# First block of a two-block transformer kernel: memory projections placed first, mixed heads in pairs, last modulation chunks in the feed-forward

## The reference

```python
mod = silu(c) @ w_ada + b_ada                      # 6 x 1024: shift1, scale1, gate1, shift2, scale2, gate2
h = rms_norm(x, g_norm1) * (1 + scale1) + shift1
sb_q, sb_k, sb_v, gq, gk, gv, gg, gf = split(h @ w_in)         # 3 x 512, 2 x 256, 2 x 512, 16
# stick-breaking, for each of 8 heads of 64, s < t:
z = q k^T / 8
weights = exp(log_sigmoid(z) + reverse exclusive cumsum over s of log_sigmoid(-z))
o_sb = weights @ v
# gated linear attention, chunks of 64, 4 heads: state = decay * state + k_dec^T v;  o = q state
o_gla = rms_norm(o_gla) * g_gla_out * silu(gg)
x = x + (1 + gate1) * (concat(o_sb, o_gla) @ w_out)
h2 = rms_norm(x, g_norm2) * (1 + scale2) + shift2
u = causal_depthwise_conv(h2 @ w_up); val, gte = split(u)
x = x + (1 + gate2) * ((val * silu(gte)) @ w_down)
# second block, used later:  mkv = rms_norm_2(mem, mem_norm_g) @ mem_kv   for layers a and b
```

## Time and profile before

| | us |
|---|---|
| median of 3 runs | 1300.62 (1298.9 to 1304.4) |
| profiled execution | 1301.19 |
| its span | 1299.4 |
| PE busy | 1150.4 (89%) |
| DVE busy | 803.2 (62%) |
| ACT busy | 547.0 (42%) |
| mean granted clock of PE | 0.944 of full speed |
| chain that ended last: PE, DVE, ACT | 74%, 14%, 7% |

### The profile page before, as it was taken

One profiled execution on the slowest core, in us unless ns is written; L12 is line 12 of the kernel. 1 busy time (PEld: TensorE's weight loads), 2 busy tenths in 40 slices (PEclk: granted clock), 3 DMA queues, 4 the chain that ended last, 5 costly groups with the idle time before them and its releaser, 6 DMA issues.

```text
span 1299.4 us, 24238 instructions
## 1 busy us (share of the span) xinstructions
PE 1150.4 (89%) x10670; PEld 1073.2 (83%) x10670; DVE 803.2 (62%) x1268; ACT 547.0 (42%) x768; POOL 28.4 (2%) x28
## 2 busy tenths in 40 slices
PE   3789998899999977778768999999899779999997
PEld 3789887899999976566657899999788558999997
DVE  6787665678875555655553456655666875455554
ACT  1443441456554445433332444444535224444432
POOL 0000000000000000223000000000000000000000
PEclk9988997889999988888998899999899898999999
DMA  9655553635544442110002355446315203355451
GB/s 358 231 193 195 195 194 132 238 117 194 178 139 169 165 187 100 70 60 2 36 28 73 118 196 181 159 157 205 109 41 196 98 1 130 132 192 185 134 181 54
DMA packets 30233, 185.88 MB, mean 143 GB/s; under 512 B 3360, under 2 KB 4528, under 8 KB 12720
## 3 DMA queue, kind: packets, MB, share of 16 engines
q1 hardware_dynamic: 30128, 184.34, 39.9%
HBM read 183.27 MB, written 1.05 MB: 142 GB/s over the span
## 4 chain that ended last, share of the span: by engine, by line
PE 74%; DVE 14%; ACT 7%; issue 4%; DMA 1%; SPq 0%; DVEq 0%; ACTq 0%
PE banks L308 45%; PE banks L1056 13%; ACT whi L276 3%; DVE wlo L285 3%; PE banks L305 2%; PE banks L460 1%; DMA X<-in_xT 1%; DVE ub L447 1%; DVE adac L1244 1%; PE banks L1575 1%; PE banks L1558 1%; PE banks L1234 1%; DVE ub L367 1%; PE banks L1543 1%; ACT ssb L329 0%
## 5 line engine op out<-in xcount | busy, mean ns | idle before, releaser
L285 DVE TENSOR_TENSOR wlo<-raw,whi 128x2048 fp32r<-128x2048 f32 (+4 forms) x174 | 340.5, 1958 | 215.2 <-ACT whi L276 213.6
L276 ACT ACTIVATE whi<-raw 128x2048 fp32r<-128x2048 f32 (+4 forms) x174 | 285.2, 1640 | 162.7 <-PE banks L1056 97.1
L308 PE MATMUL banks<-h_hi,whi 128*128 128x256 f32 x1632 | 237.3, 299 | 27.8 <-ACT h_hi L356 16.9
L308 PEld LDWEIGHTS banks<-h_hi,whi 128*128 128x128 f32 x1632 | 216.9, 199 | 39.0 <-issue 22.6
L308 PE MATMUL banks<-h_hi,wlo 128*128 128x256 f32 x1632 | 221.5, 290 | 2.5 <-DVE wlo L285 2.5
L308 PE MATMUL banks<-h_lo,whi 128*128 128x256 f32 x1632 | 214.6, 284 | 0.0
L308 PEld LDWEIGHTS banks<-h_hi,wlo 128*128 128x128 f32 x1632 | 210.1, 197 | 4.9 <-DVE wlo L285 2.8
L308 PEld LDWEIGHTS banks<-h_lo,whi 128*128 128x128 f32 x1632 | 202.4, 190 | 3.1 <-issue 2.1
L1056 PE MATMUL banks<-m_hi,whi 128*128 128x256 f32 x528 | 71.3, 281 | 4.9 <-ACT m_hi L1096 4.9
L1086 ACT ACTIVATE u<-u 128x256 f32<-128x256 f32 x44 | 18.4, 418 | 130.2 <-DVE u L1133 130.2
L1056 PE MATMUL banks<-m_hi,wlo 128*128 128x256 f32 x528 | 71.1, 283 | 0.0
(11 more groups left out here) (454 smaller groups left out, 1387.6 us busy)
## 6 DMA issues: line engine op xcount, KB each, us to landing
raw<-in_ada SPq DMA_DIRECT2D x24, 1024.0 KB, 4.9
raw<-in_w_up SPq DMA_DIRECT2D x22, 1024.0 KB, 4.8
raw<-in_a_gu SPq DMA_DIRECT2D x22, 1024.0 KB, 4.8
raw<-in_b_gu SPq DMA_DIRECT2D x22, 1024.0 KB, 4.8
raw<-in_w_in SPq DMA_DIRECT2D x12, 1024.0 KB, 5.9
raw<-in_w_down SPq DMA_DIRECT2D x16, 704.0 KB, 4.1
raw<-in_a_in SPq DMA_DIRECT2D x11, 1024.0 KB, 4.8
raw<-in_a_down SPq DMA_DIRECT2D x16, 704.0 KB, 4.1
```

What stands on the lines that cost most here:

```text
L276: act.activation(hi_s[k % NSPLIT][:, 0:w], raw[n % NRAW][:, 0:w], ACT.Copy).then_inc(*hi_made.tick(k))
L285: dve.tensor_tensor(lo_s[s][:, 0:w], raw[n % NRAW][:, 0:w], hi_s[s][:, 0:w].bitcast(F), SUB).then_inc(*lo_made.tick(k))
L308: i_ = pe.matmul(b[0:m, j * T:(j + 1) * T], a[:, kt * step + j * m:kt * step + j * m + m], x[:, kt, :], start=st, stop=sp)
```

## The change

- **Order of the stream and the projections.** The memory, its gain and the constants `ones` and `eps` are issued first; the four memory chunks head `ONE` (c = 0 to 3), mixed with ada 0 to 7. Then come w_in chunks 0, 2, 4, 7, w_gf, 8, 9, 6, 1, 3, 5, 10, 11 (c = 4 to 16). The first eight scaled chunks use the buffer of the gated state S1 in place of `ub`.
- **Loops.** DVE now splits chunk c+2 first and then scales ada c+3, in loops 5 to 16. `ONE_EXTRA` tells behind which piece the small matmuls stand.
- **Heads in pairs.** z, c and o handle two heads (384 columns each, 768 in all); one double bank holds scores and running sums of a pair, and a matmul with the mask replaces the multiply by `strict`. c waits for DVE's step of the same pair (`("max", p)`). Outputs go from the banks straight to `mm_hi` and `mm_lo`.
- **Gated attention.** It uses two banks only (4 and 5), go alternates between the halves, the gain is folded into the norm.
- **Evacuations.** ACT takes all banks but those of w_gf and w_in 7, 10, 11.
- **Last modulation chunks.** ada 19 is in loop 16, ada 20 to 23 (gate2) stand in the stream behind w_up 2, 6, 10, 14 and are scaled by DVE in those steps of the feed-forward; gate2 is added up at w_up 18.

The diff, cut to its core:

```diff
-WIN = [7, 12, 8, 9, 6, 0, 2, 4, 1, 3, 5, 10, 11]
+WIN = [0, 2, 4, 7, 12, 8, 9, 6, 1, 3, 5, 10, 11]
...
 def stream_order():
-    o = [("ada", i) for i in range(8)]
-    one = [("w_gf", 0) if i == 12 else ("w_in", i) for i in WIN]
-    one += [("mkv_a", 0), ("mkv_a", 1), ("mkv_b", 0), ("mkv_b", 1)]
-    o += one[:6]
-    for j in range(11):
-        o += [("ada", 8 + j), one[6 + j]]
-    o += [("ada", j) for j in range(19, 24)]
-    for name in ("w_out", "w_up", "w_down", "a_in", "a_out", "a_gu", "a_down", "kv_down", "b_in",
+    o = [("mkv_a", 0), ("mkv_a", 1), ("ada", 0), ("ada", 1), ("mkv_b", 0), ("ada", 2), ("ada", 3), ("mkv_b", 1)]
+    o += [("ada", j) for j in range(4, 8)]
+    one = [("w_gf", 0) if i == 12 else ("w_in", i) for i in WIN] + [("w_out", 0)]
+    o += one[:2]
+    for j in range(12):
+        o += [("ada", 8 + j), one[2 + j]]
+    o += [("w_out", i) for i in range(1, 4)]
+    for i in range(22):
+        o.append(("w_up", i))
+        if i % 4 == 2 and i < 16:
+            o.append(("ada", 20 + i // 4))
...
+        def scores(pe, p, first):
+            Z = zbank(p)
+            for e in range(2):
+                r = slice(64 * e, 64 * e + 64)
+                pe.matmul(Z[:, 512 * e:512 * e + 256], k1[r, p, 0:128], q1[r, p, :], start=first, stop=False)
+            for e in range(2):
+                r = slice(64 * e, 64 * e + 64)
+                pe.matmul(Z[:, 512 * e + 256:512 * e + 384], k1[r, p, 128:256], q1[r, p, 128:256], start=False, stop=False)
+            for e in range(2):
+                pe.matmul(Z[:, 512 * e:512 * e + 128], M_ID, M_SU, start=False, stop=False)
+                x = pe.matmul(Z[:, 512 * e + 256:512 * e + 384], M_ID, M_SU, start=False, stop=True)
+            return x
...
             for c in range(NM, N1 + 1):
                 if c > NM:
                     dve_evac1(dve, c - 1)
                     dve_split(dve, c + 2)
...
+                if 5 <= c <= 16:
+                    dve_ada(dve, c + 3)
+                if c == 8:
+                    dve_z(dve, 0)
+                if c == 9:
+                    dve_gate(dve)
+                if c == 10:
+                    dve_mix(dve, 0)
+                    dve_z(dve, 1)
...
+        ONE_EXTRA = {
+            (7, 1): [("z", 0)], (8, 2): [("c", 0)], (9, 1): [("o", 0), ("z", 1)], (9, 3): [("gate",)],
+            (10, 1): [("c", 1)], (10, 3): [("o", 1)], (10, 5): [("ktr",)], (11, 1): [("kv", 0)], (11, 5): [("kv", 1)],
+            (12, 3): [("go",)], (13, 3): [("gsq", 0), ("gsq", 1)], (14, 1): [("z", 2)], (14, 5): [("z", 3)],
+            (15, 1): [("c", 2)], (15, 3): [("c", 3)], (15, 5): [("o", 2)], (16, 2): [("o", 3)],
+        }
...
+            if piece == 2 and 6 <= c <= 16:
+                pe_ada(pe, c + 2)
...
                     dve_split(dve, split_k[up, i] + 3)
+                    if up == "w_up" and i % 4 == 2 and i < 16:
+                        dve_ada(dve, 20 + i // 4)
```

More of the change, by code:

```diff
@@ L508, in dve_evac1 @@
             b = bank[c % 2]
-            if (name, i) in BY_ACT:
+            if (name, i) not in BY_DVE:
                 return
@@ new lines, in act_c, with opair, pe_o @@
+        def act_c(act, p):
+            act.wait_ge(*sb_p.at(("c", p)))
+            act.activation(sW[p % NW][:, :, :], zpair(p), ACT.Exp).then_inc(*sb_a.tick(("w", p)))
+        def opair(p):
+            return bank[(6, 2, 6, 4)[p]][:, 0:256]
+        def pe_o(pe, p):
+            W, O = sW[p % NW], opair(p)
+            pe.wait_ge(*sb_a.at(("w", p)))
+            pe.wait_ge(*evac_a.at(("w_in", 4 + p // 2)))
+            if p == 2:
+                pe.wait_ge(*h_lo_made.at(("mix", 0)))
+            for n in range(2):
+                for e in range(2):
+                    h = 2 * p + e
+                    o = O[64 * e:64 * e + 64, :] if n == 0 else O[64 * e:64 * e + 64, 128:256]
+                    w = W[:, e, 0:256] if n == 0 else W[:, e, 256:384]
+                    x = pe.matmul(o, v1[:, n, 64 * h:64 * h + 64], w, start=n == 0, stop=n == 1)
+            x.then_inc(*sb_p.tick(("o", p)))
@@ L783, in act_one @@
             act.preload_act_table_set(LN_EXP)
+            act.wait_ge(*d_mem.at(0))
+            for kt in range(8):
+                act_square(act, "mem", kt, mem[:, kt, :])
+            act_split(act, 0)
+            act_rs(act, "mem", bank[5])
+            for kt in range(8):
+                act_mem_split(act, kt)
+            act_split(act, 1)
             act.wait_ge(*d_x.at(0))
@@ L826, in act_one @@
[L826 to L832 removed]
+                    act_z(act, 2)
+                if c == 15:
+                    act_z(act, 3)
+                    act_c(act, 2)
+                if c == 16:
+                    act_c(act, 3)
+                    act_mix(act, 2)
+                    act_mix_gla(act, 0)
+            act_mix(act, 3)
+            act_mix_gla(act, 1)
@@ new lines, in dve_one @@
+        def dve_one(dve):
+            for kt in range(8):
+                dve_square(dve, "mem", kt)
+            dve_split(dve, 0)
+            dve.wait_ge(*rs_a.at("mem"))
+            for kt in range(8):
+                dve_scale(dve, "mem", kt, mem, V("mem_g", 0, 8), rs_t[:, :])
+            for kt in range(8):
+                dve_mem_split(dve, kt)
+            dve_split(dve, 1)
+            dve_ada(dve, 0)
+            for kt in range(8):
+                dve_square(dve, "n1", kt)
+            dve_ada(dve, 1)
+            dve_split(dve, 2)
+            dve_ada(dve, 2)
+            dve_ada(dve, 3)
+            dve_split(dve, 3)
+            for i in range(4, 8):
@@ L929, in pe_extra @@
+        def pe_extra(pe, c, piece):
+            for e in ONE_EXTRA.get((c, piece), ()):
+                if e[0] == "z":
+                    pe_z(pe, e[1])
+                if e[0] == "c":
+                    pe_c(pe, e[1])
+                if e[0] == "o":
+                    pe_o(pe, e[1])
+                if e[0] == "gate":
                     pe_gate(pe)
-                if c == 4:
+                if e[0] == "ktr":
                     pe_ktr(pe)
-                if c == 5:
-                    pe_kv(pe, 1)
@@ L1042, in pe_ffn @@
                     pe.wait_ge(*rs_a.at(before))
+                elif f == 3 and up == "w_up":
+                    pe.wait_ge(*mod_v.at("gate2"))
                 for half in range(2):
```

555 lines of the change are left out of this document (252 added, 303 removed).

## The result

Four runs of the changed kernel gave a median of **1366.9 us** (1365.1 to 1373.4), beside 1301.1 us (1298.9 to 1304.4) for the kernel before: ratio 1.051, 95% interval 1.047 to 1.055. The forecast was 1348, the range 1312 to 1372. The profiled execution has a span of 1365.2 us (before 1299.4).

A forecast was written before the change was run, and what follows sets the result against it. PE was taken to bound loops 7 to 16, incoming data and DVE's scaling the head. Forecast: 1301.2 us before + 38.2 for the first block + 9.2 for the feed-forward = 1348.6, given as 1348; range 1312 to 1372.

The forecast's parts named there:

- The head: Start of the kernel: DVE's chain puts the first w_in matmul at 61.7 us, 21 us later, with four memory chunks done.
- The ring: Projection loops: modulation and weight chunks share four slots, freed late and issued in order, so 14.3 us a loop.
- The walk: Loops 8 to 16 through w_out, timed stop by stop: w_out ends at 291.0 us against 252.8 before, +38.2.
- The pairs: Attention heads in twos on PE: z 1.8, c 4.1, o 1.2 us, 28 us for four pairs, 6 us less PE work.
- the feed-forward: w_up with four modulation chunks moved in: 3.4 us PE work plus 5.8 us DVE shortfall, +9.2 us (3.4 to 15).
- late slot: In w_up, the next w_up but two waits for the slot a modulation scaling frees; third and fourth run short 2.8 us each.
- The sign named for this term: In the trace of after, waits in w_up of none or over 10 us would break the feed-forward term.
- After it: The rest of the kernel behind the feed-forward: nothing changes, 0 us.
- A: Rival, chance 0.11: in the first block the ring costs nothing, only second waits hold; w_out ends near 262, total 1319 us.
- second waits: First block: PE waits for DVE's extras behind the scaling, ready 8.6 us after chunk c-1, wanted after 1.9 us.
- B: Rival, chance 0.09: PE finds every input ready in the loops, w_out ends at 210, total 1262 us, faster.
- C: Rival, chance 0.08: idle in each loop keeps PE at half clock throughout from loop 8 on, +32 us, total 1380.

The follow-up runs named there:

- the kernel with all edits: Changed kernel with stream in order of use, DVE's extras first, feed-forward products one w_up chunk late, modulation chunks five w_up chunks apart: 1267.0 us, ratio 0.976.

## Why the prediction came out as it did

**The head: right.** The last early scaling ended at 58.1 (58.2), the first w_in matmul began at 61.61 (61.7), the chunk was done at 70.9 (71).

**The ring: right, as mechanism and as size.** Scalings of ada 8 to 11 end at 83.8, 92.4, 108.2 and 122.6 (83.7, 92.2, 106.5, 120.8). The first full period is 15.8, not 14.3: the second transfer of that pair had landed 8.3 us after its issue (92.82 to 101.08), the next one 6.8 (108.61 to 115.44), on both sides of the 7.3 taken. Of the waits named for ACT, those of 9 to 11 us came (10.4, 10.5, 10.0), as did that of loop 10 (2.8); in loop 15 it was 6.1, for w_out, not 1 to 3.

**The walk: right within 4 us at every stop**, the late stops always later: ada 15 191.0 (188.1), ada 16 208.4 (205.5), ada 18 237.7 (234.1), w_out's seventh row tile 269.6 (267.4), its end 292.4 (291.0). Two errors hide in that agreement and cancel, which is luck. The pairs cost PE less (below): from c(1) to the end of its chunk 10.7 us passed, not 12.4, and from c(2) 13.0, not 15.3. And a restart can cost more than the 2.5 us taken, or the 3.4 of its upper bound: behind 6.0 us of idle, from kv in loop 11 to the end of that chunk 10.8 us passed, where the prediction has 5.7 of work and 2.5 of restart, so the half clock cost 5.1 (PE timeline of after; the next loop starts at 183.29).

```profile
172.46 2.08 PE L711 MATMUL banks<-gv,g 64*128 64x256 f32 x8 [6.00 <-DVE g L699]
...
179.75 3.62 PE L313 MATMUL banks<-h_lo,whi 128*128 128x256 f32 x16
183.29 1.46 PE L711 MATMUL banks<-gv,g 64*128 64x256 f32 x8
```

**The pairs: too dear.** z 1.35, c 3.20, o 0.80 at full clock (1.8, 4.1, 1.2): 21 us for four pairs, not 28, and below the low end of 25. The Trainium skill, page TensorEngine Tiling (Array Packing), section Theoretical Speedup (up to 2x at a dimension of at most 64), had it right here: four products took 0.85 us, what two take for one head. The middle value rested on a misreading of the earlier trace rows: 1.1 us for four products where one alone takes 0.54 is not in between, it is already two at a time. Below the low end it came by c: the running sums of two heads took 1.85 us, where those of one took 1.22 before; why is open. c of the last pair, and then o of the pair before it, in the PE timeline of after:

```profile
246.39 0.59 PE L612 MATMUL banks<-sL,con 128*128 128x256 f32 x2
...
248.24 0.70 PE L563 MATMUL banks<-q,k 64*128 64x256 f32 x4
...
249.59 2.13 PE L313 MATMUL banks<-h_lo,whi 128*128 128x256 f32 x16
251.66 0.87 PE L636 MATMUL banks<-sW,v 128*64 128x256 f32 x8
252.46 2.14 PE L313 MATMUL banks<-h_hi,whi 128*128 128x256 f32 x16
```

**The step that failed: the feed-forward, +9.2, measured +24.0**, above the term's own upper end of 15. "Four chunks cost DVE 26.2 against PE's 23.4; the first has 2.6 us to spare" adds up DVE's work and its wait for the late slot, and lets PE lose only what DVE then lacks over four chunks. What it leaves out is where PE's product stands. DVE starts its part when chunk 2 is done: it waits 1.3 us for ACT, then has taps (1.8), split (2.2) and scaling (2.9) to do, and is ready 8.2 us after that chunk. PE asks for the product 5.7 us after it, behind chunk 3. So it stands 2.45 us there, at each of the four places from the first on, with the half clock behind it. The prediction makes just this sum for the first block ("ready 8.6 us after chunk c-1") and not for the feed-forward. The 5.8 us for the late slot measured 7.2. The sign named for this term did not catch it: PE's idle in w_up came to 9.7 us, within the 10, since the half clock behind the waits is no idle. The total of 1366.9 lies in the range, 5 us under its end.

**After it: right.** The +2.2 us behind w_up are no effect: over the fourteen profiled kernels, whose code is the same from there on, that part took 907.6 to 918.8 us.

**The rivals.** A's second waits were right one by one, 37.3 us in sum for the 38 listed, but w_out ended at 268.5 with the ring gone, not near 262. The waits being right, the difference lies in PE's busy time: 161.6 us, against 135.3 in the kernel with all edits, so the clock costs 26.3 more there (0.81 over the stage; a restart as in the earlier trace rows). How much of it A had put in, its text does not say. B asked whether PE could find all inputs ready; the kernel with all edits nearly does so (14.8 us of idle, most of it at w_out and the norm), ends w_out at 212.2 (210 was worked out for B) and takes 1267.0 us (1262). C did not come: PE's clock is 0.80 over the stage, not 0.5. The Trainium skill, page Perfetto Trace Analysis, section Optimization Strategy, takes a repeating gap for a possible lack of buffers; here ACT's repeating wait for a slot of the ring went with the same four slots, by order alone, so it was no lack of them.

What each part of the change is worth, then: with scaling ahead of the split and everything else as changed, w_up begins 12.0 us earlier than before (249.8 for 261.8, a shift of which some 6 can be the clock, see the last section); the swap of split and scaling costs 51.6; the feed-forward part 24.0. Moving four modulation chunks out of the kernel before brought w_up to 254.2, 247.5 and 246.9, so the 12.0 are about what that move gives by itself. What pairs and order of projections gain is hidden by the waits, and comes out with both cured: 221.1 against 246.9. That these add up (-12.0 + 51.6 + 24.0 = 63.6 of 65.8) is by construction of the runs. That the 51.6 would be as large on another first block is not shown, since ring and second wait cover one another.

## What to carry to other kernels

Where two streams share a ring of slots and one queue fills it in order, put the stream in the order in which the slots are freed: that order alone gave back 24.0 us here, and in the kernel with DVE's extras first 14.0 more than the swap on DVE did. A swap of two consumers, without a single instruction added, cost 51.6 us, by the ring and by the second wait together. When two waits each seem to be worth little, try both cures at once, since the loop keeps the period of the one that is left (24 and 18 us alone, 81 together, a quarter of it through the clock). And where work is moved beside a full engine, ask not only whether the others have time for it but how long after the last input it is ready, and place its consumer one step behind that.
